# Hybrid decoder step on one core: output projection by contraction blocks over eight open tiles, w_ada piece 12 ahead of w_in, caches behind it

## Chip, cores and metric

One NeuronCore of a Trainium2 chip. The metric is the device time of one launch in microseconds. The kernel was timed in three runs; beside them stands one profiled execution, from which all durations are read. In the text TensorE is PE, VectorE DVE, ScalarE ACT, GpSimd POOL and SyncE SP, as in the rows.

## What is computed

One decoder layer in float32 for 256 prompt tokens and 8 decode tokens (264 columns), D = 1024:

```python
mod = silu(c) @ w_ada + b_ada                    # six vectors of 1024 for each condition row
h = rmsnorm(x, g_mix) * (1 + sc1) + sh1
q_a, k_a, v_a, q_h, f_h, i_h, g_h = split(h @ w_in)
o_a = rmsnorm(sink_attention(rotary(q_a), rotary(k_a), v_a))       # 8 heads, 2 KV heads, window 128
o_h = rmsnorm(hgrn(q_h, f_h, i_h)) * silu(g_h)                      # 4 heads, state 128 x 128
x = x + gt1 * (concat(o_a, o_h) @ w_out)
h = rmsnorm(x, g_ffn) * (1 + sc2) + sh2
x = x + gt2 * moe(h)                             # top 4 of 32 experts, clamped SwiGLU
y = rmsnorm(x, g_final)
```

Beside y the kernel returns the window caches and the states, which are updated (decode) or final (prompt).

## The kernel before

The program is written by hand for each engine, in the order in which the engine runs it, with semaphores between the engines. It has two parts.

**The front** (to about 260 us) does everything up to the router. Weights come through `ring`, eight places of 8 KB a partition; `PLACES` gives the place of each chunk and SP issues the loads in a fixed order. w_ada comes in 8 + 16 chunks (`w_ada_rows(i)`, 16 pieces of 1 MB), w_in in pieces of 1 and 2 MB (`w_in_columns`), w_out in four chunks WO0 to WO3: two hold the rows of the attention half (four DMAs each), two those of the hg half (one DMA each). A load waits until its place is free: `chunks_used` counts chunks of w_in and later ones, `ada_used` chunks of w_ada that PE has used. POOL issues the small and the strided loads: caches, sinks, router bias, states, and the copies of the caches to the outputs. PE does the input projection in turns with w_ada chunks (L961), the levels of the recurrence (L1197), rotations (L1204) and attention queries (L1213), then scores, values and the recurrence.

**The output projection** has `cat`, 8 contraction steps of 128 rows: steps 0 to 3 are attention heads, 4 to 7 hg heads. `project(d)` makes one of eight output tiles (128 columns of w_out) of 264 tokens in one PSUM bank, over all 8 steps (L1456); `x1_column(d)` on DVE (L2069 to L2075) adds it to the residual, ACT squares and scales it (L833, L834), and `token_sums(d)` (L1468, L1472) adds it to router logits and sums of squares. `outer` (L1440) makes the decode states' updates, `update_states` (L2059) adds them on DVE. `att_ready` and `hg_ready` tell that the two halves of `cat` are normalised (`norm_values`, `norm_heads`); on ACT their inverse roots are Ln and Exp for the prompt (L805, L808) and Sqrt for the decode rows (L801).

**The expert loop** runs 16 pairs of experts. A pair has 12 chunks of 2 MB; eight buffers hold them (`big(c)`): 0 to 3 are the ring's places two by two, 4 and 5 lie in the arena, 6 over the decode states, 7 over the residual. The first eight are issued one by one as their memory comes free at the front's end; from chunk 8 on each waits until PE has used the chunk eight before (`load_later`):

```python
sp.wait_ge(chunks_used, turn2 * (2 * PER) + (PRE + n - BIGS + 1))
expert_chunk(n, (turn2 * 2 + n // PER) % PAIRS)
```

PE's first matmul on a chunk is the first of L1656.

Of the kernel before, what the change touches and what calls it, by code (L numbers as in the profile page):

```python
# [24 lines left out]
KT = D // P  # L25
S = 256
NB = 8
# [51 lines left out]
    6, 7, 0, 6, 7, 0, 6, 7, 0, 1, 6, 7, 0, 1, 6, 7) + (6, 7, 4, 5)  # L79
# [65 lines left out]
def hybrid_layer(nc, A, O):  # L145
    with ExitStack() as ctx:
# [236 lines left out]
        for name, b in (  # L383
# [37 lines left out]
        def _(sp):  # L421
# [50 lines left out]
            for i in range(6, 12):  # L472
                w_ada_rows(i)
            w_in_columns(Z0 + 7, 12)
            for i in range(12, 2 * N_ADA):
                w_ada_rows(i)
            w_in_columns(Z0 + 9, 15)
            for c in range(4):
                n = WO0 + c
                if c < 2:  # L480
                    sp.wait_ge(ada_used, 15 + c)
                    for i in range(2):
                        for g in range(KV):
                            sp.dma_start(two(chunk(n))[64 * g:64 * g + 64, i, :], w_out_a[2 * c + i, g]).then_inc(full[place(n)], 16)
                else:
                    sp.wait_ge(chunks_used, Z0 + 9)
                    sp.dma_start(two(chunk(n)), w_out_h[c - 2]).then_inc(full[place(n)], 16)
# [58 lines left out]
        def _(pool):  # L546
# [15 lines left out]
            pool.wait_ge(chunks_used, Z0 + 5)  # L562
# [78 lines left out]
        def _(act):  # L641
# [185 lines left out]
            root(r_att[:, S:NTOK], "asd", bank("asd")[:, 0:NB], AW)  # L827

# [103 lines left out]
        def _(pe):  # L932
# [37 lines left out]
            give(mm, "cT")  # L970
            def turn_x(k):
# [457 lines left out]
            give(turn(out[:, 0:64], pvr[0:64, :], 64), "dT")  # L1429
            pe.wait_ge(sem("hg_squares"), 3)  # L1430
# [16 lines left out]
            def project(d):  # L1447
                out = take(f"wo{d}")
                for k in range(KT):
                    if d == 0:  # L1450
                        landed(WO0 + k // 2)
                        if k == 0:
                            pe.wait_ge(sem("att_ready"), 1)
                        if k == 4:
                            pe.wait_ge(sem("hg_ready"), 3)
                    mm = pe.matmul(out[:, 0:NTOK], lhsT=two(chunk(WO0 + k // 2))[:, k % 2, P * d:P * (d + 1)], rhs=cat[:, k, :],  # L1456
                                   start=(k == 0), stop=(k == KT - 1))
                give(mm, f"wo{d}")

            def token_sums(d):  # L1460
# [9 lines left out]
                if d == 6:  # L1470
                    mm.then_inc(chunks_used, 4)
# [18 lines left out]
            project(0)  # L1490
            project(1)
            outer(1, ("ow0", "ow1", "ow2", "ow3"))
            pe.wait_ge(sem("router_row"), 2)
            out = take("cwr")
            pe.matmul(out[:, 0:E], lhsT=ones[0:E, :], rhs=bdiag[0:E, :], start=True, stop=True)
            give(pe.matmul(out[0:NB, E:2 * E], lhsT=cw[0:E, 1:1 + NB], rhs=ident[0:E, 0:E], start=True, stop=True), "cwr")
# [209 lines left out]
        def _(dve):  # L1706
# [323 lines left out]
            dve.tensor_scalar(bdiag[0:E, :], ident[0:E, 0:E], cw[0:E, 0:1], None, ALU.mult).then_inc(sem("router_row"), 1)  # L2030
            wait_emptied(dve, "qkb")
# [13 lines left out]
            norm_heads(0)  # L2045
            norm_values(0, S)
            norm_heads(1)
            wait_emptied(dve, "asd")
            link(dve.reciprocal(r_att[:, S:NTOK], r_att[:, S:NTOK]))
            norm_values(S, NB).then_inc(sem("att_ready"), 1)  # L2050
            wait_emptied(dve, "hsd")
            link(dve.reciprocal(r_hgd, r_hgd))
            dve.tensor_tensor(cat[:, 4:8, S:NTOK], cat[:, 4:8, S:NTOK], r_hgd, ALU.mult).then_inc(sem("hg_ready"), 1)

# [7 lines left out]

            dve.wait_ge(sem("states_full"), 16 * NB)
            update_states(0, ("ou0", "ou1", "ou2", "ou3"))

# [11 lines left out]
            x1_column(0)  # L2077
            x1_column(1)
            update_states(1, ("ow0", "ow1", "ow2", "ow3"))
            wait_filled(dve, "cwr")  # L2080
            dve.tensor_copy(brow, bank("cwr")[:, 0:E])
            dve.tensor_copy(brow_s[0:NB, :], bank("cwr")[0:NB, E:2 * E]).then_inc(emptied("cwr"), 1)
            for d in range(2, KT):
                x1_column(d)
# [248 lines left out]
```

## Time and profile before

| | us |
|---|---|
| median of 3 runs | 1194.55 (1194.54 to 1194.88) |
| profiled execution, time | 1195.86 |
| its span, first to last instruction | 1194.1 |
| PE busy in the span | 1109.4 (93%) |
| DVE / ACT / POOL busy | 335.9 / 165.7 / 55.6 |
| DMA | 461.65 MB, mean 387 GB/s |
| mean granted clock of PE | 0.985 of 2.4 GHz |

The profile's page cuts the span into 40 slices of 30 us. The DMA moved 167 to 350 GB/s in slices 2 to 8 and about 430 from slice 11 to the last but one. Busy time is the time with an instruction running, whether or not it waits for a pipeline; what an engine waited for stands in the rows behind a bracket, as idle time and what ended it. A float32 matmul that is no transpose counts twice in the trace (16 projection matmuls are x32).

### The profile page before, as it was taken

What the parts mean: (1) busy time and instruction counts of PE and PEld (TensorE: products, weight loads), DVE (VectorE), ACT (ScalarE), POOL (GpSimd) and SP (SyncE); (2) the same over time, 40 slices, a digit from 0 to 9 for tenths busy, and PEclk for the clock granted to TensorE, in tenths of its full rate; (3) what the DMA queues carried; (4) which work ended last, traced back from release to release, by engine and by line L of the source; (5) the groups of instructions that cost most, each with busy time, mean ns of one, the idle gap of its engine ahead of it and who ended that gap; (6) DMA issues with size and microseconds to landing.
All of it is one profiled execution on the core that took longest, in us unless ns stands there. A gap on an engine that the chain in (4) does not pass through costs nothing.

```text
span 1194.1 us, 14038 instructions
## 1 busy us (share of the span) xinstructions
PE 1109.4 (93%) x5465; PEld 439.8 (37%) x5465; DVE 335.9 (28%) x753; ACT 165.7 (14%) x317; POOL 55.6 (5%) x86
## 2 busy tenths in 40 slices
PE   7997999999999999989898989898989898989896
PEld 3554577753332333323232323232323232323222
DVE  4133545351322232222222221212121212121214
ACT  3230153230010101000100010001000100000003
POOL 1111201210000000000000000000000000000000
PEclk9997998999999999999999999999999999999999
DMA  9879554689999999999999999999999999999994
GB/s 364 296 306 350 167 194 175 232 313 397 430 428 430 431 430 430 430 430 430 431 431 431 428 431 430 430 432 431 429 431 430 430 431 431 429 430 429 431 430 194
DMA packets 49128, 461.65 MB, mean 387 GB/s; under 512 B 6657, under 2 KB 7873, under 8 KB 22202
## 3 DMA queue, kind: packets, MB, share of 16 engines
q1 hardware_dynamic: 42512, 445.17, 89.2%
q0 software_dynamic: 5600, 13.13, 3.2%
q10 hardware_dynamic: 986, 2.95, 0.7%
q8 instruction: 20, 0.33, 0.1%
q14 instruction: 10, 0.08, 0.0%
HBM read 460.30 MB, written 5.78 MB: 390 GB/s over the span
## 4 chain that ended last, share of the span: by engine, by line
PE 57%; DMA 40%; DVE 2%; issue 1%; POOL 0%; ACT 0%; SPq 0%; DVEq 0%
PE bank L1656 27%; DMA arena<-in_w_up 17%; DMA ring<-in_w_up 17%; PE bank L1536 6%; PE bank L1680 4%; DMA ring<-in_w_ada 3%; DMA arena<-in_w_down 3%; PE bank L1456 3%; PE bank L937 2%; PE bank L1649 2%; PE bank L1116 1%; PE bank L1248 1%; PE bank L1039 1%; PE bank L1056 1%; PE bank L1542 1%; PE bank L961 1%
## 5 line engine op out<-in xcount | busy, mean ns | idle before, releaser
L1656 PE MATMUL bank<-arena 128*64 128x512 f32 x1024 | 240.0, 600 | 11.4 <-DMA arena<-in_w_up 10.9
L1656 PE MATMUL bank<-ring,arena 128*64 128x512 f32 x1024 | 240.0, 601 | 9.9 <-DMA ring<-in_w_up 8.7
L1656 PEld LDWEIGHTS bank<-arena 128*64 128x64 f32 x1024 | 67.3, 136 | 164.4 <-issue 149.5
L1656 PEld LDWEIGHTS bank<-ring,arena 128*64 128x64 f32 x1024 | 66.0, 136 | 163.6 <-issue 137.5
L1680 PE MATMUL bank<-arena 128*64 128x512 f32 x512 | 114.6, 596 | 9.1 <-DMA arena<-in_w_down 9.1
L1680 PE MATMUL bank<-ring,arena 128*64 128x512 f32 x512 | 114.6, 596 | 9.1 <-DMA ring<-in_w_down 9.1
L2229 DVE TENSOR_SCALAR arena<-bank 128x256 f32<-128x256 f32 x64 | 24.2, 419 | 275.2 <-PE bank L1656 275.2
L1536 PE MATMUL bank<-arena,mods 128*128 128x512 f32 (+1 forms) x204 | 93.7, 630 | 0.9 <-DVE arena L2256 0.9
L891 ACT ACTIVATE arena<-arena 128x512 f32<-128x512 f32 x32 | 20.2, 630 | 493.6 <-DVE arena L2229 493.6
L2218 DVE TENSOR_TENSOR x<-x,bank 128x512 f32<-128x512 f32 x64 | 44.0, 687 | 144.5 <-PE bank L1536 144.5
L937 PE MATMUL bank<-const,arena 128*128 128x128 f32 (+3 forms) x348 | 51.0, 288 | 23.2 <-DMA ring<-in_w_down 7.6
L2248 DVE COPY arena<-bank 64x512 f32<-64x512 f32 x30 | 20.6, 688 | 164.2 <-PE bank L1680 164.2
L1680 PEld LDWEIGHTS bank<-arena 128*64 128x64 f32 x512 | 36.4, 137 | 80.9 <-issue 69.6
L1680 PEld LDWEIGHTS bank<-ring,arena 128*64 128x64 f32 x512 | 35.2, 137 | 82.2 <-issue 61.5
L937 PEld LDWEIGHTS bank<-const,arena 128*128 128x128 f32 (+3 forms) x348 | 40.8, 165 | 54.8 <-issue 44.9
L612 POOL DMA_INDIRECT arena<-h_rows,idx x15 | 15.0, 998 | 810.4 <-DVE idx L2163 751.9
L1536 PEld LDWEIGHTS bank<-arena,mods 128*128 128x128 f32 (+1 forms) x204 | 22.8, 161 | 69.2 <-issue 68.7
L902 ACT ACTIVATE arena<-bank 64x512 f32<-64x512 f32 x32 | 18.9, 591 | 162.7 <-PE bank L1680 162.7
L1649 PE MATMUL bank<-arena 32*64 32x512 f32 x256 | 34.8, 613 | 0.0
L1456 PE MATMUL bank<-arena,ring 128*128 128x264 f32 x128 | 33.0, 417 | 1.2 <-DVE arena L2014 1.2
L898 ACT ACTIVATE arena<-bank 128x512 f32<-128x512 f32 x32 | 19.0, 595 | 79.0 <-PE bank L937 79.0
L1456 PEld LDWEIGHTS bank<-arena,ring 128*128 128x128 f32 x128 | 25.7, 205 | 8.1 <-issue 3.6
(338 smaller groups left out, 799.3 us busy)
## 6 DMA issues: line engine op xcount, KB each, us to landing
ring<-in_w_up SPq DMA_DIRECT2D x64, 2048.0 KB, 34.1
arena<-in_w_up SPq DMA_DIRECT2D x64, 2048.0 KB, 34.2
ring<-in_w_down SPq DMA_DIRECT2D x32, 2048.0 KB, 33.6
arena<-in_w_down SPq DMA_DIRECT2D x31, 2048.0 KB, 33.4
ring<-in_w_ada SPq DMA_DIRECT2D x16, 1024.0 KB, 10.1
ring<-in_w_ada SPq DMA_DIRECT2D x16, 512.0 KB, 10.9
ring<-in_w_in SPq DMA_DIRECT2D x3, 2048.0 KB, 12.8
ring<-in_w_in SPq DMA_DIRECT2D x5, 1024.0 KB, 12.4
```

The lines of the kernel that those rows point to most:

```text
L891: act.activation(sg, glu, ACT.Sigmoid, scale=ALPHA).then_inc(sem("sig_ready"), 1)
L898: act.activation(gT[e], B[6 + e][:, :], ACT.Copy).then_inc(sem("gT_copied"), 1)
L902: act.activation(ysb[r, e, :], B[4 + e][r, :], ACT.Copy).then_inc(sem("y_kept" if last else "y_copied_a"), 1)
L937: return pe.transpose(out, in_, ident[0:rows, 0:rows])
L1456: mm = pe.matmul(out[:, 0:NTOK], lhsT=two(chunk(WO0 + k // 2))[:, k % 2, P * d:P * (d + 1)], rhs=cat[:, k, :], start=(k == 0), stop=(k == ...
L1536: return pe.matmul(out, lhsT=Wc[:, cols], rhs=rows, start=first, stop=True, skip_group_check=True)
L1649: pe.matmul(B[2 * e + c % 2][64 * a:64 * a + 64, :], lhsT=own_row[32 * c:32 * c + 32, e, :], rhs=bias[32 * c:32 * c + 32, :], start=False, ...
L1656: mm = pe.matmul(B[2 * e + c % 2][64 * a:64 * a + 64, :], lhsT=xTe[:, k, 64 * e:64 * e + 64], rhs=big(PER * s + n)[:, r, 512 * c:512 * (c ...
L1680: mm = pe.matmul(B[4 + e][64 * a:64 * a + 64, :], lhsT=gT[e].rearrange("p (j a t) -> p j a t", j=4, a=2)[:, k % 4, k // 4, :], rhs=big(PER ...
L2218: dve.tensor_tensor(acc, acc, part, ALU.add).then_inc(sem("sum_added"), 1)
L2229: ins = dve.tensor_scalar(glu[:, 256 * b:256 * (b + 1)], u[:, :, 0], LIMIT, None, ALU.min)
L2248: dve.tensor_copy(ysb[dst, 1 - e, :], B[4 + e][src, :]).then_inc(sem("y_copied_d"), 1)
```

## The change

On SP, w_ada piece 12 is issued ahead of the w_in columns Z0+7 instead of behind them; w_out's hg half is issued ahead of its attention half, and the two halves trade places in the ring. Expert chunks 4 and 5 no longer wait for `hg_ready`; chunk 2 waits for 2 of the 4 counts that the projection gives, ahead of chunk 6. On POOL the caches and all behind them wait for the use of w_ada piece 12. On PE two 128x256 matmuls on constants are added at the front, the router-row matmuls ("cwr") move ahead of the decode norms, and the projection is done by contraction steps: 0 to 3 for tiles 0 to 3, outer products, 4 and 5 for tiles 0 to 3, 0 to 3 and then 4 and 5 for tiles 4 to 7, and 6 and 7 tile by tile with the token sums. The eight tiles have a bank each. On DVE and ACT the norms are put in another order.

```diff
-    6, 7, 0, 6, 7, 0, 6, 7, 0, 1, 6, 7, 0, 1, 6, 7) + (6, 7, 4, 5)
+    6, 7, 0, 6, 7, 0, 6, 7, 0, 1, 6, 7, 0, 1, 6, 7) + (4, 5, 6, 7)
...
-                ("wo0", 2), ("wo1", 3), ("ow0", 4), ("ow1", 5), ("ow2", 6), ("ow3", 7), ("cwr", 1), ("wo2", 2), ("rt", 0),
-                ("wo3", 3), ("wo4", 2), ("wo5", 3), ("h00", 4), ("h10", 5), ("wo6", 2), ("wo7", 3), ("h01", 4), ("h11", 5),
+                ("wo0", 0), ("wo1", 1), ("wo2", 2), ("wo3", 3), ("ow0", 4), ("ow1", 5), ("ow2", 6), ("ow3", 7), ("wo4", 4), ("wo5", 5),
+                ("wo6", 6), ("wo7", 7), ("rt", 0), ("h00", 4), ("h10", 5), ("h01", 4), ("h11", 5),
...
-            for i in range(6, 12):
+            for i in range(6, 13):
                 w_ada_rows(i)
             w_in_columns(Z0 + 7, 12)
-            for i in range(12, 2 * N_ADA):
+            for i in range(13, 2 * N_ADA):
                 w_ada_rows(i)
             w_in_columns(Z0 + 9, 15)
-            for c in range(4):
+            for c in (2, 3, 0, 1):
                 n = WO0 + c
                 if c < 2:
-                    sp.wait_ge(ada_used, 15 + c)
+                    sp.wait_ge(chunks_used, Z0 + 9)
...
                 else:
-                    sp.wait_ge(chunks_used, Z0 + 9)
+                    sp.wait_ge(ada_used, 13 + c)
...
             sp.wait_ge(sem("att_ready"), 1)
-            sp.wait_ge(sem("hg_ready"), 1)
             sp.wait_ge(sem("st_stored"), 16)
             for c in (4, 5):
                 expert_chunk(c, 0)
+            sp.wait_ge(chunks_used, PRE - 2)
+            expert_chunk(2, 0)
             sp.wait_ge(sem("states_stored"), 16 * NB)
             expert_chunk(6, 0)
             sp.wait_ge(chunks_used, PRE)
-            for c in (2, 3):
-                expert_chunk(c, 0)
+            expert_chunk(3, 0)
...
-            pool.wait_ge(chunks_used, Z0 + 5)
+            pool.wait_ge(ada_used, 13)
             pool.dma_start(vc, A["cache_v_win"][0].rearrange("b s g d -> s b (g d)")).then_inc(sem("cache_full"), 16)
...
-            inverse_root(r_hg[0])
             inverse_root(r_att[:, 0:S])
-            inverse_root(r_hg[1])
...
             root(r_att[:, S:NTOK], "asd", bank("asd")[:, 0:NB], AW)
+            inverse_root(r_hg[0])
+            inverse_root(r_hg[1])
...
+            for _ in range(2):
+                pe.matmul(B[1][:, 0:NEARLY], lhsT=ident, rhs=const[:, 0:NEARLY], start=True, stop=True)
...
-            project(0)
-            project(1)
+            for d in range(4):
+                project(d, 0, 4)
             outer(1, ("ow0", "ow1", "ow2", "ow3"))
...
+            for d in range(4):
+                project(d, 4, 6)
+            for d in range(4, KT):
+                mm = project(d, 0, 4)
+            release(mm, 2)
+            for d in range(4, KT):
+                project(d, 4, 6)
+            project(0, 6, KT)
+            project(1, 6, KT)
             token_sums(0)
-            for d in range(2, 6):
-                project(d)
+            for d in range(2, 7):
+                project(d, 6, KT)
                 token_sums(d - 1)
             for t in range(2):
                 turn_columns(f"h{t}0", x1s, t, 0, paired=True)
-            for d in range(6, KT):
-                project(d)
-                token_sums(d - 1)
+            project(7, 6, KT)
+            token_sums(6)
...
+            dve.wait_ge(sem("powers"), 1)
+            norm_values(0, S)
...
-            norm_heads(0)
-            norm_values(0, S)
-            norm_heads(1)
...
+            wait_filled(dve, "cwr")
+            dve.tensor_copy(brow, bank("cwr")[:, 0:E])
...
             dve.wait_ge(sem("states_full"), 16 * NB)
             update_states(0, ("ou0", "ou1", "ou2", "ou3"))
+            norm_heads(0)
+            norm_heads(1)
+            wait_emptied(dve, "hsd")
...
+            update_states(1, ("ow0", "ow1", "ow2", "ow3"))
```

SP's loads from w_ada piece 6 to expert chunk 7 (L464 are pieces of w_ada, L453 columns of w_in, L484 and L487 the two halves of w_out, L493 expert chunks), before:

```order
L464 DMA ring<-in_w_ada 128x2048 x6
L453 DMA ring<-in_w_in 128x8x512
L464 DMA ring<-in_w_ada 128x2048 x4
L453 DMA ring<-in_w_in 128x8x512
L484 DMA ring<-in_w_out 64x1024 x8
L487 DMA ring<-in_w_out 128x2x1024 x2
L493 DMA ring<-in_w_up 128x4096 x2
L493 DMA arena<-in_w_up 128x4096 x3
L493 DMA ring<-in_w_up 128x4096 x2
L493 DMA arena<-in_w_up 128x4096
```

and in the change:

```order
L464 DMA ring<-in_w_ada 128x2048 x7
L453 DMA ring<-in_w_in 128x8x512
L464 DMA ring<-in_w_ada 128x2048 x3
L453 DMA ring<-in_w_in 128x8x512
L487 DMA ring<-in_w_out 128x2x1024 x2
L484 DMA ring<-in_w_out 64x1024 x8
L493 DMA ring<-in_w_up 128x4096 x2
L493 DMA arena<-in_w_up 128x4096 x2
L493 DMA ring<-in_w_up 128x4096
L493 DMA arena<-in_w_up 128x4096
L493 DMA ring<-in_w_up 128x4096
L493 DMA arena<-in_w_up 128x4096
```

One w_ada piece went ahead of the w_in columns, the halves of w_out changed places, and an expert chunk in the ring went ahead of the one over the states.

PE from the decode norms (L1432, L1318) to the second token sums, before; L1440 are outer products, L1495 and L1496 the router row, L1456 projection matmuls:

```order
L1432 MATMUL bank<-arena,const 128x32
L1318 MATMUL bank<-arena,const 128x8 x4
L1440 MATMUL bank<-mods,arena 128x128 x16
L1456 MATMUL bank<-arena,ring 128x264 x16
L1440 MATMUL bank<-mods,arena 128x128 x16
L1495 MATMUL bank<-arena,const 128x32
L1496 MATMUL bank<-const,small 8x32
L1468 MATMUL bank<-arena,x 32x264
L1472 MATMUL bank<-arena,const 32x264
L1456 MATMUL bank<-arena,ring 128x264 x8
L1468 MATMUL bank<-arena,x 32x264
L1472 MATMUL bank<-arena,const 32x264
```

and in the change, where the router row is L1435 and L1436, the norms L1439 and L1321, outer products L1447, the projection L1464 and token sums L1478 and L1482:

```order
L1435 MATMUL bank<-arena,const 128x32
L1436 MATMUL bank<-const,small 8x32
L1439 MATMUL bank<-arena,const 128x32
L1321 MATMUL bank<-arena,const 128x8 x4
L1447 MATMUL bank<-mods,arena 128x128 x16
L1464 MATMUL bank<-arena,ring 128x264 x16
L1447 MATMUL bank<-mods,arena 128x128 x16
L1464 MATMUL bank<-arena,ring 128x264 x36
L1478 MATMUL bank<-arena,x 32x264
L1482 MATMUL bank<-arena,const 32x264
L1464 MATMUL bank<-arena,ring 128x264 x2
L1478 MATMUL bank<-arena,x 32x264
```

Between two token sums stand 2 projection matmuls now, 8 before.

ACT's inverse roots (L808), decode squares (L823, L825) and decode roots (L801) up to the first tile's squares (L833), before:

```order
L808 ACT_TABLE_LOAD
L808 ACTIVATE x<-x 128x512
L808 ACTIVATE x<-x 128x256
L808 ACTIVATE x<-x 128x512
L823 ACTIVATE arena<-arena 128x4x8
L825 ACTIVATE arena<-arena 128x4x8
L801 ACT_TABLE_LOAD
L801 ACTIVATE x<-bank,small 128x32
L801 ACTIVATE x<-bank,small 128x8
L833 ACTIVATE arena<-arena 128x264
```

and in the change, where the squares are L821 and L823:

```order
L808 ACT_TABLE_LOAD
L808 ACTIVATE x<-x 128x256
L821 ACTIVATE arena<-arena 128x4x8
L823 ACTIVATE arena<-arena 128x4x8
L801 ACT_TABLE_LOAD
L801 ACTIVATE x<-bank,small 128x32
L801 ACTIVATE x<-bank,small 128x8
L808 ACT_TABLE_LOAD
L808 ACTIVATE x<-x 128x512 x2
L833 ACTIVATE arena<-arena 128x264
```

The two hg roots stand behind the decode roots with a table load of their own; a further load stands ahead of the router's square roots (L856), where there was none.

## Rows read from the trace of the kernel before

**Rows 1.** Busy time by stretch: PE, PEld, DVE, ACT, POOL; PEclk, DMA share, GB/s.

```profile
264.00:285.00 21.00, 21.00 (x87) 5.59 (x85) 6.22 (x11) 0.63 (x1) 1.04 (x2) 1.00 0.98 370
450.00:1170.00 720.00, 666.58 (x3004) 214.99 (x3004) 167.49 (x327) 62.20 (x104) 10.89 (x11) 1.00 1.01 430
```

**Rows 2.** DMA issues at 183 us and at 264 us, to landing.

```profile
ring<-in_w_up SPq DMA_DIRECT2D x1, 2048.0 KB, 7.8
...
ring<-in_w_down SPq DMA_DIRECT2D x1, 2048.0 KB, 8.9
```

**Rows 3.** Timeline of PE, 93 to 132 us: start, us, line, tiles, [idle before].

```profile
95.35 1.92 PE L961 MATMUL bank<-ring,arena 128*32 128x512 f32 x16
...
103.34 1.06 PE L961 MATMUL bank<-ring,arena 128*32 128x512 f32 x8
113.24 1.93 PE L961 MATMUL bank<-ring,arena 128*32 128x512 f32 x8 [8.83 <-DMA ring<-in_w_ada]
...
125.42 1.93 PE L961 MATMUL bank<-ring,arena 128*32 128x512 f32 x16
```

**Rows 4.** Busy time by stretch, columns as in rows 1.

```profile
113.00:124.00 11.00, 10.76 (x48) 6.51 (x50) 4.21 (x8) 1.06 (x1) 0.00 (x0) 0.51 0.31 130
199.00:209.00 10.00, 8.81 (x52) 7.29 (x52) 9.03 (x30) 1.46 (x3) 0.57 (x1) 0.50 0.56 206
210.00:247.00 37.00, 36.84 (x222) 27.00 (x221) 13.38 (x63) 9.17 (x23) 6.36 (x9) 1.00 0.59 206
```

**Rows 5.** Timeline of SP's DMA issues, 80 to 90 us.

```profile
85.19 1.28 SPq L464 DMA_DIRECT2D ring<-in_w_ada  x3
86.51 1.10 SPq L453 DMA_DIRECT2D ring<-in_w_in  x1
89.34 3.26 SPq L464 DMA_DIRECT2D ring<-in_w_ada  x1
```

**Rows 6.** Timeline of POOL, 84 to 110 us, and DMA issues to landing.

```profile
85.46 0.95 POOL L563 DMA_DIRECT2D arena<-in_cache_v_win  x1 [25.97 <-PE bank L1213]
...
small<-in_attn_sinks POOLq DMA_DIRECT2D x8, 0.0 KB, 10.8
```

**Rows 7.** Timeline of DVE, 110 to 160 us.

```profile
118.88 0.70 DVE L1852 COPY_PREDICATED arena<-const,bank 128x512 f32<-128x512 uint32 x1 [14.81 <-PE bank L1197]
...
147.31 0.17 DVE L1905 TENSOR_TENSOR small<-small 128x8 f32<-128x8 f32 x1
```

**Rows 8.** Timeline of PE, 183 to 264 us.

```profile
203.54 10.13 PE L1456 MATMUL bank<-arena,ring 128*128 128x264 f32 x32 [1.19 <-DVE arena L2014]
...
219.87 3.83 PE L1456 MATMUL bank<-arena,ring 128*128 128x264 f32 x16
...
243.59 0.41 PE L1472 MATMUL bank<-arena,const 128*32 128x264 f32 x1
...
260.11 3.65 PE L1656 MATMUL bank<-ring,arena 128*64 128x512 f32 x16 [0.44 <-ACT arena L880]
```

**Rows 9.** Timeline of PE, 0 to 24 us.

```profile
10.54 0.47 PE L937 MATMUL bank<-const,arena 128*128 128x128 f32 x1 [0.49 <-DMA arena<-in_hg_lb_logits]
```

**Rows 10.** Timeline of DVE, 183 to 215 us.

```profile
200.34 1.67 DVE L2014 SCALAR_TENSOR_TENSOR arena<-arena,small,x 128x256 f32<-128x256 f32 x4
...
202.75 0.64 DVE L2014 SCALAR_TENSOR_TENSOR arena<-arena,small,x 128x8 f32<-128x8 f32 x4
...
203.91 4.22 DVE L2059 SCALAR_TENSOR_TENSOR arena<-arena,bank 128x128 f32<-128x128 f32 x16
```

**Rows 11.** Timelines of DVE and ACT, 215 to 240 us: tile 2.

```profile
219.41 0.48 DVE L2069 SCALAR_TENSOR_TENSOR arena<-bank,arena 128x256 f32<-128x256 f32 x1 [0.21 <-PE bank L1456]
...
220.53 0.49 ACT L834 ACTIVATE arena<-arena 128x256 f32<-128x256 f32 x1
```

**Rows 12.** Timeline of ACT, 183 to 264 us.

```profile
198.62 1.28 ACT L801 ACT_TABLE_LOAD   x1
...
245.19 0.26 ACT L856 ACTIVATE small<-bank,small 128x2 f32<-128x2 f32 x1 [0.55 <-PE bank L937]
```

More of the change, by code:

```diff
@@ L1429, in _ @@
             give(turn(out[:, 0:64], pvr[0:64, :], 64), "dT")
+            pe.wait_ge(sem("router_row"), 2)
+            out = take("cwr")
+            pe.matmul(out[:, 0:E], lhsT=ones[0:E, :], rhs=bdiag[0:E, :], start=True, stop=True)
+            give(pe.matmul(out[0:NB, E:2 * E], lhsT=cw[0:E, 1:1 + NB], rhs=ident[0:E, 0:E], start=True, stop=True), "cwr")
             pe.wait_ge(sem("hg_squares"), 3)
@@ L1445, in _, with project @@
             outer(0, ("ou0", "ou1", "ou2", "ou3"))
[L1447 to L1450, printed above, removed]
+            def project(d, first, last):
+                out = take(f"wo{d}") if first == 0 else bank(f"wo{d}")
+                for k in range(first, last):
+                    if d == 0 and k % 2 == 0:
                         landed(WO0 + k // 2)
[L1452 to L1455, printed above, removed]
+                    if d == 0 and k == 0:
+                        pe.wait_ge(sem("att_ready"), 1)
+                    if d == 0 and k == 4:
+                        pe.wait_ge(sem("hg_ready"), 3)
                     mm = pe.matmul(out[:, 0:NTOK], lhsT=two(chunk(WO0 + k // 2))[:, k % 2, P * d:P * (d + 1)], rhs=cat[:, k, :],
-                                   start=(k == 0), stop=(k == KT - 1))
-                give(mm, f"wo{d}")
+                                   start=(k == 0), stop=(k == KT - 1), skip_group_check=True)
+                if last == KT:
+                    give(mm, f"wo{d}")
+                return mm
             def token_sums(d):
@@ L1470, in token_sums @@
                 if d == 6:
-                    mm.then_inc(chunks_used, 4)
+                    mm.then_inc(chunks_used, 2)
                 mm = pe.matmul(out[E:2 * E, 0:NTOK], lhsT=ones[:, 0:E], rhs=squares_1[:, d % 4, :], start=(d == 0), stop=(d == KT - 1),
@@ L1488, in turn_columns @@
                     give(mm, name)
-            project(0)
-            project(1)
+            for d in range(4):
+                project(d, 0, 4)
             outer(1, ("ow0", "ow1", "ow2", "ow3"))
[L1493 to L1496, printed above, removed]
+            for d in range(4):
[7 more added lines that the diff above has]
+            project(1, 6, KT)
             token_sums(0)
-            for d in range(2, 6):
-                project(d)
+            for d in range(2, 7):
+                project(d, 6, KT)
                 token_sums(d - 1)
@@ L2044, in _ @@
             dve.tensor_tensor(km, wide(krows.unsqueeze(1), 1, NB), wide(C("same").unsqueeze(2), 2, P), ALU.mult).then_inc(sem("km_ready"), 1)
-            norm_heads(0)
-            norm_values(0, S)
-            norm_heads(1)
[L2048 to L2053, printed above, removed]
             def update_states(i, names):
@@ L2061, in update_states @@
                     ins.then_inc(emptied(names[hd]), 1)
+            wait_filled(dve, "cwr")
+            dve.tensor_copy(brow, bank("cwr")[:, 0:E])
+            dve.tensor_copy(brow_s[0:NB, :], bank("cwr")[0:NB, E:2 * E]).then_inc(emptied("cwr"), 1)
+            wait_emptied(dve, "asd")
+            link(dve.reciprocal(r_att[:, S:NTOK], r_att[:, S:NTOK]))
+            norm_values(S, NB).then_inc(sem("att_ready"), 1)
             dve.wait_ge(sem("states_full"), 16 * NB)
             update_states(0, ("ou0", "ou1", "ou2", "ou3"))
+            norm_heads(0)
+            norm_heads(1)
+            wait_emptied(dve, "hsd")
+            link(dve.reciprocal(r_hgd, r_hgd))
+            dve.tensor_tensor(cat[:, 4:8, S:NTOK], cat[:, 4:8, S:NTOK], r_hgd, ALU.mult).then_inc(sem("hg_ready"), 1)
+            update_states(1, ("ow0", "ow1", "ow2", "ow3"))
             def x1_column(d):
@@ L2075, in x1_column @@
                 dve.tensor_tensor(x1s[:, d, S:NTOK], xT[:, d, S:NTOK], s2T[:, d, 1:9], ALU.mult).then_inc(sem("x1s_ready_s"), 1)
[L2077 to L2083, printed above, removed]
+            for d in range(KT):
                 x1_column(d)
```

2 rows, old and new, of the table bank_of are left out of this document.

## The prediction

> **What bounds the kernel now.** I read the busy table of two stretches first. From 450 us to nearly the end the DMA engines are full (share 1.01, 430 GB/s) and TensorE is busy only 666.58 of 720 us: it waits for experts' weights. Between 264 and 285 us, just behind the start of the expert loop, it is the other way round: TensorE is busy all the time and the DMA moves 370 GB/s [rows 1]. The DMA list says why. Eight buffers of 2 MB hold experts' weights, and chunk 8 can be asked for only when TensorE has used chunk 0. The one asked for behind 263 us lands 8.9 us later; one that had the DMA nearly to itself, at 183, took 7.8 us [rows 2]. So almost nothing is queued when the loop starts, and from there 184 chunks come one behind the other: the end is the loop's start plus a constant. **What moves the loop's first matmul (260.11 us [rows 8]) moves the end by as much; what only lets weights land earlier ahead of it moves nothing.**
>
> So I read TensorE's list ahead of 260 us for time that is not work. The largest piece is a wait of 8.83 us, up to 113.24, for a piece of w_ada [rows 3]. Behind it the granted clock is at its lower level, 1.2 GHz: 0.51 from 113 to 124 us. A second low stretch, 0.50 from 199 to 209 us, lies around the start of the output projection [rows 4], which TensorE starts 1.19 us late, waiting for VectorE [rows 8].
>
> **The missed piece.** SyncE issues three pieces of w_ada at 85.19, 2 MB of w_in at 86.51 and the missed piece, w_ada 12, behind it at 89.34 [rows 5]. POOL starts 1 MB of caches at 85.46 [rows 6], and behind them sinks and 1 MB of copies in DRAM. In the change the piece goes ahead of w_in, and the caches wait until TensorE has used it. Four pieces of 1.05 MB from 85.2 us, at 400 GB/s (between the two rates of [rows 1]), take 10.5 us; with some 3 us of latency (7.8 less 4.9 for 2 MB [rows 2]) the piece lands by 99. TensorE wants it at 104.4 (103.34 and 1.06 [rows 3]). The pieces behind it are asked for when chunks 9, 10 and 11 are used, as before.
> The gain is the wait, 8.83 us, and the slow clock behind it. From 95.35 to 103.34 TensorE did two pieces, a level, a rotation and queries in 7.99 us at full clock; one piece less (0.93) is 7.06. From 113.24 to 125.42 it took 12.18 for that [rows 3], 5.12 more. Together **-13.95 us**. VectorE doesn't take the stall over: it waited 14.81 us for TensorE's next level meanwhile [rows 7].
>
> **What is moved down.** POOL's queue is released at about 105.3 instead of 85.46. Two caches and ten small issues at 0.95 us at most, and 10.8 us to landing [rows 6], put the sinks at 128. VectorE wants them at 147.31 [rows 7], in the change 13.95 earlier, at 133.4: 5 us to spare. The states behind them on POOL wait for an inner product of TensorE that moves by 13.95 too. On SyncE the hg half of w_out now comes first, and the attention half, 8 DMAs, waits for the first state product; behind it stand expert chunks 0 and 1, wanted only in the loop. No term.
>
> **The two matmuls at the front.** They have 256 columns each; by the projection's (8 of 264 columns in 3.83 us [rows 8]) that is 0.95 us together. TensorE waited 0.49 us for a load just behind [rows 9], which hides half. Bounds 0 and 0.95; I take **+0.4**.
>
> **The projection.** VectorE does the prompt's attention values (1.67 us) ahead of the decode rows' steps, and the two hg scalings (0.7 each, as between the two rows of values) behind the first state update. The decode values' end, att_ready, was 203.39 [rows 10]; without two scalings ahead it is 202.0. TensorE's outer products ended at 202.35 (203.54 less 1.19 [rows 8]) and come 0.4 later, for the values ahead of them. So the projection starts at about 202.8, **0.7 earlier**. The first state update (4.22 us [rows 10]) and the scalings end by 208.5 and are wanted behind 16 matmuls, at 213; the second update, behind the second outer products, ends by 218.3, and the first tile of the second four, at 217.9, needs only its first quarter.
> The 64 matmuls are the same. But before, a whole tile (3.83 us) lay between a tile's end and its sums; now 2 matmuls do, 0.95 us. From a tile's end (VectorE starts 0.1 behind it, at 219.41) to ScalarE's scaled column (221.02) are 1.7 us [rows 11]. Step by step, with 0.6 for a pair of sums: the first pair waits 0.8, tiles 2 and 4 0.25 each, and tile 6 0.55, because ScalarE copies two banks (0.5 each, as its column [rows 11]) ahead of its column: **+1.85**. The two router-row matmuls move into a gap, **-0.5** (at most 0.95 by the projection's). At the last sums (243.59 before [rows 8]) this comes to **+0.65**; bounds -1.2 with no waits, and +1.9 with neither the start nor the gap.
>
> **The tables of ScalarE.** Its two hg roots (Exp) now come behind the Sqrt of the decode rows, which adds two table loads of 1.28 us [rows 12]. The first ends before 203.4, covered by the 4.22 us of state update; without that cover its 1.28 would show in the second block. The second stands ahead of the router's square roots at 245.19, which had waited 0.55 us for TensorE [rows 12]. It hides this much and adds **+0.7** to the way to the loop; bounds 0 and 1.28.
> The Trainium skill (ScalarE: Activation LUTs, What ACT_TABLE_LOAD costs) speaks against such an order: it wants calls grouped by table and gives some 2.66 us for a switch, a drain included. By that the sum would be 1.38 higher. The rows show a load of 1.28 us alone, and they decide.
>
> **DMA behind the block order.** Chunk 2 can be issued when eight tiles have used the attention half, chunks 4 and 5 1.4 us earlier, chunk 6 in order behind chunk 2, chunk 3 where it was. All lie ahead of the first release at 264, where nobody waits for them: 0. Chunk 7 stays tied to the last transposes.
>
> **Sum.** -13.95 + 0.4 + 0.65 + 0.7 = -12.2. The profiled execution took 1195.86 us, 1.31 above the median of the runs, 1194.55: it would take 1183.7, and on the runs' scale **1182.4 us**.
>
> **Rivals.**
> *The second slow stretch shrinks.* Without the 1.19 us ahead of the projection the clock may stay up or come back sooner. Between 203.54 and 209 some 5.4 us ran at half: -2.7, 1179.7. Against: the waits ahead of 199 stay. 0.13.
> *It gets longer, or part of the stall stays* (the low clock through the rest of the first 16 matmuls, 4.6 us to 213.67 [rows 8]; or another piece late). About 1187. For: the low stretch behind 113 lasted over 10 us [rows 4]. 0.13.
> *The DMA is the bound already,* and the change does not bring what it moves: an earlier loop only waits for chunks. 1194.5. Against: 370 GB/s and 8.9 us behind the start [rows 1, 2]. 0.03.
> *Slower: the clock falls in the last block.* TensorE pauses there between tiles and goes through eight open banks. Its work is eight tiles of 0.95 and 0.6 us, 12.4; at the lower level 12.4 more, less the 1.85 of waits that it swallows, +10.5: 1192.9. If it lasts through the 16.5 us from the last sums to the loop [rows 8], of which I take a third as TensorE's own, +5.5: 1198. It ends on the slow side from 12.2 us of TensorE work at the lower clock. Against: from 210 to 247 us, with the same matmuls, the clock was 1.00 [rows 4], and the four pauses are under 1 us each. 0.06.
> The Trainium skill (TensorE: Matmul & The Clock Gate, A second HAM failure mode) tells of kernels whose groups cycle through PSUM banks with short pauses, and whose clock then swings; by that rule it would be this rival. The trace of before, which pauses less there, does not show it.
>
> **Numbers.** The forecast has 0.63; 0.02 is left for what I don't see. The range goes from the first rival less its small terms' bounds, 1178.6, to the second with the table's bound, 1188.0; it leaves out the other two. About 0.2%, 2.4 us, is what a measurement of this kernel can tell from no change. Faster 0.93, same 0.03, slower 0.04.
>
> **What would show it.** No wait for w_ada over 1 us on TensorE and a granted clock of 1.00 from 104 to 124 us; the loop's first matmul some 12 us before 260.11; short waits of the sums for ScalarE at the projection's end; a table load ahead of the router's roots; landing times near 8 us at the loop's start. I am wrong if the first matmul moves by 12 us and the end by much less (a queue at the DMA after all), if VectorE's maxima wait for the sinks, or if the clock is at 0.5 anywhere from the second block to the loop.

## The result and the profile after

The changed kernel took 1181.41 us (median of four runs, 1178.35 to 1182.54) beside 1194.55 of the kernel before, a ratio of 0.9887 with a 95% interval of 0.9867 to 0.9908. Six later runs gave 1182.34 and 0.9899 (0.9881 to 0.9916). The forecast was 1182.4. The profiled execution took 1182.54 us, its span 1180.7.

TensorE's timeline from 94 us on, of the changed kernel, answers to [rows 3] and [rows 8] (start, us, line, tiles, [idle before]):

```profile
94.81 1.92 PE L961 MATMUL bank<-ring,arena 128*32 128x512 f32 x16
102.80 1.92 PE L961 MATMUL bank<-ring,arena 128*32 128x512 f32 x16
104.65 2.00 PE L1200 MATMUL bank<-arena 128*128 128x64 f32 x16
...
187.81 9.12 PE L1464 MATMUL bank<-arena,ring 128*128 128x264 f32 x32
...
215.27 0.38 PE L1478 MATMUL bank<-arena,x 128*32 128x264 f32 x1 [1.02 <-DVE arena L2093]
227.20 0.38 PE L1478 MATMUL bank<-arena,x 128*32 128x264 f32 x1 [0.75 <-ACT arena L834]
229.05 0.39 PE L1482 MATMUL bank<-arena,const 128*32 128x264 f32 x1
235.26 1.60 PE L1539 MATMUL bank<-arena,const 128*128 128x32 f32 x12 [2.50 <-DVE arena L2124]
239.04 7.77 PE L1569 MATMUL bank<-mods,arena 128*128 128x128 f32 x48
247.68 3.65 PE L1670 MATMUL bank<-ring,arena 128*64 128x512 f32 x16 [0.44 <-ACT arena L880]
```

The missed piece is one of the 16 records at 102.80, and no wait is left there. The loop starts at 247.68 instead of 260.11, 12.43 earlier (forecast 12.2). The stretches, with the columns of [rows 1] and [rows 4]:

```profile
104.00:124.00 20.00, 20.00 (x137) 12.00 (x130) 11.82 (x23) 3.79 (x6) 13.97 (x22) 1.00 0.82 297
184.70:191.30 6.60, 6.60 (x46) 5.63 (x46) 5.14 (x21) 3.76 (x6) 0.00 (x0) 0.50 0.63 207
192.00:236.00 44.00, 39.55 (x232) 28.75 (x230) 17.89 (x77) 13.54 (x30) 7.94 (x11) 1.00 0.70 259
236.00:243.00 7.00, 7.00 (x41) 5.43 (x41) 6.15 (x24) 1.17 (x2) 2.22 (x5) 0.53 0.41 122
450.00:1150.00 700.00, 648.29 (x2918) 208.90 (x2917) 161.75 (x314) 59.97 (x100) 10.88 (x11) 1.00 1.01 430
```

The clock is up from 104 to 124, where it was 0.51 for 11 us. It is at the lower level for 6.6 us around the projection's start (10 before, [rows 4]), and for most of 236 to 243, in the router's work behind the projection. There the kernel before had 3.4 us of it, behind a wait of 1.79:

```profile
249.26 1.34 PE L1525 MATMUL bank<-arena,const 128*128 128x32 f32 x12 [1.79 <-DVE arena L2112]
```

```profile
250.50:253.50 3.00, 3.00 (x20) 1.90 (x19) 2.86 (x8) 1.07 (x2) 0.00 (x0) 0.50 1.02 437
```

The steady stretch has the same 430 GB/s.

ScalarE's timeline behind the projection answers to [rows 12], POOL's and SP's at the missed piece to [rows 6] and [rows 5]:

```profile
229.88 1.28 ACT L856 ACT_TABLE_LOAD   x1
231.18 0.26 ACT L856 ACTIVATE small<-bank,small 128x2 f32<-128x2 f32 x1
```

```profile
105.05 0.95 POOL L563 DMA_DIRECT2D arena<-in_cache_v_win  x1 [45.58 <-PE bank L961]
```

```profile
84.65 4.48 SPq L464 DMA_DIRECT2D ring<-in_w_ada  x4
89.17 0.43 SPq L453 DMA_DIRECT2D ring<-in_w_in  x1
```

The table load stands ahead of the roots, the caches start 20 us later, and the four pieces go ahead of w_in.

To compare kernels, TensorE's way to the loop is cut at three rows. A is the start of the last pair of w_ada pieces ahead of the missed one's (95.35 in [rows 3], 94.81 above), B the time from there to the projection, C from there to the last sums (the last of their rows: 243.84 before, 0.25 behind the one in [rows 8]; 229.05 above), D from there to the loop's first matmul, E the rest of the span. Each line is one profiled execution; the median is that of the kernel's runs, and the ratio is to runs of the kernel before beside them.

| kernel | A | B | C | D | E | median us | ratio, interval |
|---|---|---|---|---|---|---|---|
| before | 95.35 | 108.19 | 40.30 | 16.27 | 933.99 | 1194.55 | 1 |
| changed | 94.81 | 93.00 | 41.24 | 18.63 | 933.02 | 1181.41 | 0.9887 (0.9867 to 0.9908) |
| changed again | 95.10 | 93.40 | 41.70 | 17.10 | 933.40 | 1182.34 | 0.9899 (0.9881 to 0.9916) |
| piece and caches alone | 92.28 | 94.19 | 39.41 | 14.87 | 936.35 | 1178.88 | 0.9872 (0.9854 to 0.9890) |
| piece alone | 94.36 | 104.10 | 40.53 | 16.33 | 933.38 | 1188.86 | 0.9952 (0.9933 to 0.9971) |
| caches alone | 91.81 | 94.20 | 39.39 | 14.87 | 933.73 | 1176.26 | 0.9863 (0.9837 to 0.9888) |
| the rest alone | 91.90 | 105.95 | 40.35 | 18.42 | 933.18 | 1196.11 | 1.0010 (0.9993 to 1.0028) |
| hg roots together | 92.44 | 92.66 | 40.19 | 17.87 | 933.54 | 1176.07 | 0.9844 (0.9815 to 0.9872) |
| busy wait | 94.50 | 93.17 | 41.06 | 15.66 | 933.41 | 1181.31 | 0.9895 (0.9878 to 0.9913) |
| half blocks | 90.73 | 93.25 | 37.59 | 17.28 | 933.55 | 1178.56 | 0.9874 (0.9856 to 0.9892) |
| half blocks, roots | 94.58 | 92.95 | 38.62 | 17.85 | 933.30 | 1174.99 | 0.9835 (0.9788 to 0.9881) |
| half blocks, roots, busy | 93.57 | 93.25 | 38.28 | 15.18 | 934.92 | 1174.91 | 0.9831 (0.9813 to 0.9849) |
| changed, warm front | 90.31 | 93.25 | 40.31 | 18.41 | 933.22 | 1177.24 | 0.9881 (0.9858 to 0.9904) |
| all together | 90.19 | 92.66 | 37.43 | 15.04 | 933.58 | 1172.05 | 0.9834 (0.9802 to 0.9866) |

C and D hold two things: the work, and how long the clock was low in it. TensorE is busy for nearly all of C (40.14 of 40.30 us before, 39.29 of 41.24 in the changed kernel), so the time at the lower level (0.50) may be counted half. That time is 5.6 us of C before, 3.6 in the changed kernel and 1.6 in "half blocks". Counted half, it leaves C at full clock: 37.5 us in all four profiles without blocks, 39.5 in all six with eight open tiles, 36.8 in all four with half blocks, each within 0.05. What C differs by otherwise is the clock.

### The profile page after: what moved, and what is told of

Same layout as the page of the kernel before. It is cut to its first block, busy times and chain, and to the rows that moved or that the text cites. A ratio compares the mean times of both kernels' runs of the same rounds, so it can differ in the third digit from the quotient of the medians.

```text
span 1180.7 us, 14048 instructions
## 1 busy us (share of the span) xinstructions
PE 1105.9 (94%) x5469; PEld 439.2 (37%) x5469; DVE 335.9 (28%) x753; ACT 168.3 (14%) x319; POOL 55.6 (5%) x86
## 4 chain that ended last, share of the span: by engine, by line
PE 62%; DMA 35%; DVE 2%; issue 1%; ACT 0%; SPq 0%; ACTq 0%; DVEq 0%
PE bank L1670 28%; DMA arena<-in_w_up 17%; DMA ring<-in_w_up 14%; PE bank L1550 6%; PE bank L1694 5%; PE bank L937 3%; DMA arena<-in_w_down 3%; PE bank L1464 3%; PE bank L1663 2%; PE bank L1119 2%; PE bank L961 1%; PE bank L1059 1%; PE bank L1216 1%; PE bank L1251 1%; PE bank L1042 1%; PE bank L1200 1%
## 5 line engine op out<-in xcount | busy, mean ns | idle before, releaser
L1464 PE MATMUL bank<-arena,ring 128*128 128x264 f32 x128 | 32.3, 408 | 0.0
L1464 PEld LDWEIGHTS bank<-arena,ring 128*128 128x128 f32 x128 | 24.9, 200 | 6.6 <-issue 2.4
```

## The experiments

**Piece and caches, each alone and both.** The kernel before, with one edit of the change or two:

```diff
-            for i in range(6, 12):
+            for i in range(6, 13):
...
-            pool.wait_ge(chunks_used, Z0 + 5)
+            pool.wait_ge(ada_used, 13)
```

> The kernel before with the missed piece ahead of w_in and the caches behind it, and nothing else of the change. Theory (the stall and its slow clock are the whole gain, the projection's part costs a little): the loop's first matmul comes 14 to 14.6 us before 260.11, at about 245.5 to 246, and the time is 1180 to 1181 us, as fast as the whole change or up to 2 us faster. Rival (the contraction in blocks brings a share of the gain): over 1184 us, and a loop start behind 249.

Both together take B from 108.19 to 94.19, 14.00 less (the terms of the stall and its slow clock said 13.95). C and D fall too, by 0.89 and 1.40. The low clock around the projection's start lasts as long as before, 10.2 us, but begins 6.4 us ahead of the projection instead of 4.6, so that less of it lies in C; in D the clock stays at 1.00. At 1178.88 this is no slower than the whole change. Its loop started at 240.75, earlier than expected, partly because A was 3.07 shorter; its E is 1.4 to 3.3 longer than all the others, which stays unexplained.

> The kernel before with the piece ahead of w_in alone; the caches stay where they were. Theory (the sum on record: four pieces of 1.05 MB, here with 1 MB of caches and 1 MB of copies beside them, 6.2 MB at 400 GB/s from 85.2 us and 3 us of latency, so landed by 98 to 104 us; TensorE wants the piece at about 104): the wait for w_ada is under 1 us, the clock stays up, and the time is within 1 us of the kernel with both moves, about 1180.5. Rival (the caches are what delays the piece): a wait of 2 us or more with the clock at its lower level behind it, 1184 to 1192 us.

This expectation missed: 1188.86, the rival's range. TensorE's timeline with the piece alone:

```profile
102.35 1.92 PE L961 MATMUL bank<-ring,arena 128*32 128x512 f32 x16
...
114.49 1.06 PE L961 MATMUL bank<-ring,arena 128*32 128x512 f32 x8 [4.08 <-DMA ring<-in_w_ada]
116.94 1.94 PE L961 MATMUL bank<-ring,arena 128*32 128x512 f32 x8 [1.38 <-DMA ring<-in_w_ada]
118.80 3.68 PE L1197 MATMUL bank<-arena 128*128 128x64 f32 x16
```

The piece itself is in time, at 102.35. The next two, which SP issues at 95.48, are late by 5.46 us together: the stall has moved on to them, and the clock has fallen behind it (3.68 us for the level's 16 matmuls, 2.00 at full clock).

> The kernel before with the caches behind the missed piece alone; the piece stays behind w_in. Theory (what lies ahead of the piece decides, 3 pieces, 2 MB of w_in and the piece are 6.3 MB, 15.7 us at 400 GB/s and 3 us of latency from 85.2: landed at about 104): a wait of 0 to 2 us is left in place of 8.83, and the time is 1180 to 1186 us, by whether the clock falls. Rival (w_in ahead of the piece is the whole delay): a wait of 5 us or more and 1188 to 1194 us.

This one missed too, on the good side: 1176.26 in place of 1180 to 1186. The caches alone do it, with no wait, and B, C and D as with both. So it is the caches and copies in the middle of the stream of pieces that made one late, and the piece's place ahead of w_in adds nothing to the time once they are gone. Which of the queue's transfers does it was not tried: all of them moved together. The margin is thin. The piece is issued at 85.80, as before behind w_in, and lands 14.6 us later (23.9 before), at 100.4; TensorE wants it 0.3 us later, in the middle of the row at 99.80. In the changed kernel it lands at 97.0 and is wanted at 103.7. TensorE's timeline with the caches alone:

```profile
99.80 1.92 PE L961 MATMUL bank<-ring,arena 128*32 128x512 f32 x16
101.66 2.00 PE L1197 MATMUL bank<-arena 128*128 128x64 f32 x16
...
186.01 9.22 PE L1456 MATMUL bank<-arena,ring 128*128 128x264 f32 x32 [0.99 <-DVE arena L2014]
...
230.83 1.22 PE L1525 MATMUL bank<-arena,const 128*128 128x32 f32 x12 [1.80 <-DVE arena L2112]
...
233.29 6.10 PE L1555 MATMUL bank<-mods,arena 128*128 128x128 f32 x48
```

The 48 matmuls of the router's stretch take 6.10 us here, 7.77 in the changed kernel.

**The rest alone.** The changed kernel with those two hunks undone, the signs turned.

> The changed kernel with the piece and the caches back in their old places: the contraction in blocks, the order of w_out, the tables and the front matmuls alone. Theory (they cost a little): the wait of about 8.8 us for w_ada and the slow clock behind it are back, the last sums come within 0.7 us of 243.59, the loop starts at 260 to 262.5, and the time is 1194.5 to 1197 us, by the terms on record 1196.3. Rival (the blocks bring a gain of their own): under 1193 us.

As expected by the time, 1196.11, no gain: the stall is back (8.70), D is 18.42. The loop's start, 256.62, is earlier than expected, because A is 3.45 and B 2.24 less than before. The rows behind the stall show most of B's part:

```profile
109.66 1.94 PE L961 MATMUL bank<-ring,arena 128*32 128x512 f32 x8 [8.70 <-DMA ring<-in_w_ada]
...
120.58 1.92 PE L961 MATMUL bank<-ring,arena 128*32 128x512 f32 x16
```

From the missed piece to the next pair it is 10.92 us, 12.18 before: the clock came back sooner, 1.26. With 0.13 from the wait, 0.85 is left for the projection's earlier start (forecast 0.7). So without the stall's cure the blocks are worth nothing; beside it they cost, by the rows of "changed" and "piece and caches alone", -1.19 in B, +1.83 in C and +3.76 in D, 4.40 together, and by those of "changed again" 3.73. Of D's 3.76, 3.4 is the clock, low there for 6.8 us in the one profile and not at all in the other. The intervals of the ratios overlap, so the runs alone do not show this cost.

**What D is made of.** First the order of ScalarE's roots put back:

```diff
+            inverse_root(r_hg[0])
+            inverse_root(r_hg[1])
             act.wait_ge(sem("o_ready"), 1)
...
-            inverse_root(r_hg[0])
-            inverse_root(r_hg[1])
```

> The changed kernel with ScalarE's two hg roots back ahead of the decode rows' roots, so without the two added table loads. The stretch from the last sums to the loop's first matmul took 18.63 us in the changed kernel, 16.27 before and 14.87 in the two runs without the stall and without the blocks. Theory (the loads cost what was measured, 0.5, and no more): 17.9 to 18.2 us, the wait ahead of the ranks' matmuls near 1.8 in place of 2.50, the clock low all the same behind it, and a time 0.5 to 0.7 us below the changed kernel's. Rival (the longer wait is what lets the clock fall): near 15 us, the clock at 1.00 through the stretch, 3 to 4 us faster. Second rival (the hg roots wait on the path at the projection's start): the projection starts later by up to 1 us and takes the gain back.

D lost 0.76 and the wait is 1.80 again, but the clock fell behind it all the same: the 12 matmuls take 1.87 us, 1.22 with the caches alone.

```profile
230.73 1.87 PE L1539 MATMUL bank<-arena,const 128*128 128x32 f32 x12 [1.80 <-DVE arena L2124]
```

So the length of this one wait does not decide. The runs gained more (1176.07) than these rows explain.

Then dummy matmuls in that wait:

```diff
-            pe.wait_ge(sem("chosen_ready"), 1)
             out = take("rank")
+            for _ in range(5):
+                pe.matmul(out[:, 256:512], lhsT=ident, rhs=const[:, 0:NEARLY], start=True, stop=True)
+            pe.wait_ge(sem("chosen_ready"), 1)
```

> The changed kernel with five dummy matmuls of 256 columns (some 2.3 us at the higher clock) in the wait of 2.50 us ahead of the ranks' matmuls; nothing is left out. Theory (TensorE's idle time there is what lets the clock fall): the granted clock stays at 1.00 behind it, the 48 matmuls take 6.1 us instead of 7.77, and the stretch from the last sums to the loop 15.5 to 16 us instead of 18.63: about 3 us faster than the changed kernel. Rival (the pauses of the last tiles, ahead of it, have decided already): the clock falls all the same, the dummies take up to 4.6 us and the stretch 18.6 to 21.

TensorE's timeline with them:

```profile
232.28 2.35 PE L1537 MATMUL bank<-const 128*128 128x256 f32 x10
234.95 1.22 PE L1541 MATMUL bank<-arena,const 128*128 128x32 f32 x12 [0.32 <-DVE arena L2126]
...
237.42 6.10 PE L1571 MATMUL bank<-mods,arena 128*128 128x128 f32 x48
```

The clock stays up, the 48 matmuls take 6.10 and D is 2.97 less, as the theory said. The median of the four runs is 1181.31 nevertheless, not below the changed kernel's. The profiled execution bears the theory out; a gain in the time is not shown.

**The thin last block.** Blocks for the first four tiles only, with SyncE's chunk 6 ahead of chunk 2:

```diff
             for d in range(4):
-                project(d, 4, 6)
...
+                project(d, 4, KT)
             token_sums(0)
...
+            project(4, 0, KT)
+            token_sums(1)
...
+            release(project(7, 0, 4), 2)
+            project(7, 4, KT)
             token_sums(6)
```

> The changed kernel with blocks for the first four tiles alone: their attention halves, the second outer products, their other halves, and then tiles 4 to 7 whole, one behind the other, with the sums a tile behind as before. Projection start to last sums took 41.24 us in the changed kernel, 39.4 in the runs without blocks and stall. Theory (the thin last block costs its waits, and its pauses let the clock fall behind it): 39 to 39.6 us, no wait of the sums over 0.2 us, and from the last sums to the loop 15 to 17 us instead of 18.63; together 3.5 to 5.5 us faster than the changed kernel, about 1176 to 1178. Rival (the wait of 2.50 us alone lets the clock fall): the stretch behind the last sums stays at 18 to 18.7 and only 1.8 us are gained.

C is 37.59, lower than the theory's range and 3.65 less than with all eight open; no sum waits more than 0.16. At full clock it is 2.7 less than with eight open tiles and 0.7 less than without blocks; the rest is that the clock was low for 1.6 us of it, 3.6 in the changed kernel. D stays above 17 and the clock falls in it, so the fall does not need the thin block. Next, this edit and that of the roots together:

> The same with the hg roots ahead of the decode rows' roots, so without the added table loads. Theory: another 0.5 to 0.7 us, the stretch from the last sums to the loop at 14.9 to 16.3 us, as without blocks, and the projection's start not later than in the changed kernel by more than 0.5: the fastest of the four, 1175 to 1177.5. Rival: the roots delay the decode rows' values and the projection starts up to 1 us later, so no gain against the run with loads.

The median, 1174.99, is in the theory's range, but the runs lie between 1170.87 and 1180.98. In the profile D is 17.85 with the clock at its lower level behind a wait of 1.80, the same wait behind which it stayed up in "caches alone".

And with dummies as above, `range(4)` in place of `range(5)`:

> Blocks for the first four tiles alone, the hg roots ahead of the decode rows' roots, and four dummy matmuls (1.9 us) in the wait ahead of the ranks' matmuls. Theory: from the pieces ahead of the missed one to the loop 93 us to the projection's start, 38 to 38.6 to the last sums and 14.9 to 15.2 to the loop: 146 to 147 us in place of 152.9, so some 6 us faster than the changed kernel on the same chip, about 1173 to 1176. Rival (the clock falls elsewhere in their place): over 149 us.

B, C and D add up to 146.71, as expected, and D is 15.18 with the clock up. But at the loop's start the first 16 matmuls take 5.35 us instead of 3.65, and E is 1.5 longer: the clock fell there instead. The median, 1174.91, does not differ from the kernel's without dummies.

**The front.** The changed kernel again, as it is, and with work for TensorE ahead of its first load (`zeros_made` is counted up by the clearing of `rest`):

```diff
+            pe.wait_ge(sem("zeros_made"), 1)
+            for _ in range(5):
+                pe.matmul(B[1][:, 0:NEARLY], lhsT=rest[:, 0:P], rhs=rest[:, 0:NEARLY], start=True, stop=True)
             pe.wait_ge(sem("ident_full"), 16)
```

> The changed kernel once more, beside the next two on the same chip. It is there for the spread of its runs and for a second profile of it. Theory (its runs differ by when the clock rises at the front: the modulation's first transposes of TensorE come at 21.2 to 21.9 us or at 24.8 to 25.2 in the profiles so far, 3.5 us apart): runs in two groups some 3.5 us apart, 1178 and 1182, and in the profile 152.9 us within 1 from the pieces ahead of the missed one (94.81 in the first profile) to the loop's first matmul. Rival (the spread comes of the weights' stream): the stretch from the loop's first matmul to the end differs by 3 us from 933.0.

> The changed kernel with five matmuls of 256 columns on cleared data from about 1.6 us on, while TensorE waits for its first constants up to 6.6; nothing is left out. Theory (the clock at the front rises after TensorE has been at work for some time, so work ahead of the first load brings it forward): the modulation's first transposes at 18 to 21.5 us in place of 25.2 or 21.3, the runs within 2 us of each other, and the median 2 to 5 us below the changed kernel's. Rival (the front waits for its loads, the pieces of w_ada): the transposes stay at 21 or later and the median is within 1.5 us.

Of the changed kernel again, five of six runs lie between 1181.63 and 1183.25 and one at 1177.33; E is as before, so the weights' stream is not what differs between profiles. Behind the same wait of 2.50 us the clock is low for 3.4 us this time, 6.8 in the first profile, and the 48 matmuls of the router's stretch take

```profile
239.85 6.54 PE L1569 MATMUL bank<-mods,arena 128*128 128x128 f32 x48
```

where they had taken 7.77; D is 1.53 less. The front of the changed kernel, and that with the early work:

```profile
7.53 2.07 PE L972 MATMUL bank<-const 128*128 128x256 f32 x4
...
16.34 1.94 PE L988 MATMUL bank<-ring,arena 128*32 128x256 f32 x16
...
25.22 0.44 PE L937 MATMUL bank<-const,mods 128*128 128x128 f32 x2 [0.51 <-ACT mods L650]
```

```profile
1.58 4.63 PE L967 MATMUL bank<-arena 128*128 128x256 f32 x10 [1.58 <-DVE arena L1735]
...
14.30 1.07 PE L991 MATMUL bank<-ring,arena 128*32 128x256 f32 x16
...
19.74 0.44 PE L937 MATMUL bank<-const,mods 128*128 128x128 f32 x2 [0.50 <-ACT mods L650]
```

The same 16 matmuls take 1.94 in one and 1.07 in the other, as at the clock's two levels, and the modulation's transposes come 5.5 us earlier; A is 4.50 less. But "half blocks", which has no early work, has the fast rate as early:

```profile
19.83 0.44 PE L937 MATMUL bank<-const,mods 128*128 128x128 f32 x2 [0.50 <-ACT mods L650]
```

Over the twelve profiles without early work these transposes lie between 19.83 and 25.33 us. The two with it (19.74 here, 19.61 below) are the earliest of all, but do not show by themselves that the early work is the cause. Four of the six runs are at 1176.2 to 1177.3, but two are at 1183.2; the intervals of the two ratios overlap. An effect on the time is likely and not shown.

The last kernel has both, the half blocks with roots and dummies and this front:

> The last kernel with the five matmuls on cleared data ahead of the first load as well. Theory: the pieces ahead of the missed one at 90.3 us as with the warm front alone, 93.25 from there to the projection, 38.3 to the last sums, 14.9 to 15.2 to the loop, 933.0 to 933.6 behind it (1.5 more if the clock falls at the loop's start again): a span of 1169.9 to 1172, a time of 1171.7 to 1173.8 and a median below both the changed kernel's and the last kernel's. Rival (a low stretch that is taken away at one place comes back at another): a median of 1175 or more, with the clock at its lower level somewhere between 180 us and the loop's start for longer than the 6 us around the projection.

TensorE's timeline of the last kernel:

```profile
19.61 0.44 PE L937 MATMUL bank<-const,mods 128*128 128x128 f32 x2 [0.50 <-ACT mods L650]
...
182.85 7.98 PE L1467 MATMUL bank<-arena,ring 128*128 128x264 f32 x32
...
223.74 1.89 PE L1539 MATMUL bank<-const 128*128 128x256 f32 x8
...
228.19 6.10 PE L1573 MATMUL bank<-mods,arena 128*128 128x128 f32 x48
235.32 3.65 PE L1674 MATMUL bank<-ring,arena 128*64 128x512 f32 x16 [0.60 <-ACT arena L880]
```

Five runs from 1170.67 to 1174.11, median 1172.05: every one below every run of the changed kernel. By its median it is the fastest here, 9 to 10 us ahead of the changed kernel, by the ratios 6 to 8; by the ratio it does not differ from the two kernels with half blocks and roots. A, B, C and D are as forecast within 0.9.

## Why the prediction was right, and where not

The total was right, and it rested on what it named: the loop's start moves the end. Over loop starts from 235.32 to 260.11 us E is 933.0 to 934.9 in all profiles but one (936.35). The DMA was no bound ahead of it; the chunk asked for at 251.59 landed 9.2 us later, 8.9 before [rows 2].

By the cuts, forecast against changed less before, and the same from the second profile of the changed kernel:

| | forecast | changed | changed again |
|---|---|---|---|
| A | +0.4 | -0.54 | -0.25 |
| B | -14.65 | -15.19 | -14.79 |
| C | +1.35 | +0.94 | +1.40 |
| D | +0.7 | +2.36 | +0.83 |
| sum | -12.2 | -12.43 | -12.81 |

In the first profile the sum is nearer than its parts, which is luck. (The range's upper end comes to 1187.6 by the terms it names, not 1188.0.)

- **The missed piece, -13.95: right** in size (-14.00 with its two edits alone), and it landed at 97.0 (forecast: by 99). The prediction did not say which edit carries it; the expectations did, and were wrong. Without the caches' move the next two pieces are 5.46 us late, and with that move alone the piece need not go ahead. What the caches cost the pieces behind the missed one was in neither.
- **What is moved down, no term: right.** POOL was released at 105.05 (forecast 105.3), and no engine on the way waited for it.
- **The two front matmuls, +0.4: it did not last.** They took 1.86 us, at the slow rate, and put the first w_ada matmuls at 12.83 (12.40 before), but the modulation's transposes stand at 25.22 and 25.23. A's -0.54 arises behind: a wait of 0.43 us for a w_ada piece, at 76.71 before, is not there. Between profiles A differs by up to 5 us by when the slow rate at the front ends (19.6 to 25.3 us for the modulation's transposes).
- **The projection, +0.65: its parts were mis-sized.** The start came 0.8 to 1.2 earlier than with piece and caches alone, not 0.7. The waits of the sums were 1.95 us together (1.02, 0.09, 0.09 and 0.75 by TensorE's timeline), 1.85 forecast. But C at full clock grew by 2.0, not 1.35; where the other 0.6 lies was not traced. Against it stands less slow clock in C, 3.55 us in place of 5.61, which gives back 1.0: the first rival come true at about a third of its 2.7. That makes C's +0.94.
- **The tables, +0.7: right for the load; what failed is the stretch around it, taken as fixed.** The load stands at 229.88, and the wait behind it grew from 1.79 to 2.50, 0.71. The rows show the load at 1.28 and the root 0.02 behind its end. The Trainium skill's larger price (ScalarE: Activation LUTs, What ACT_TABLE_LOAD costs, 2.66 us by its figures) is not what they show. D grew by 2.36 in the first profile because the clock was low for 6.8 us in place of 3.4 in it, which costs 1.7, and by 0.83 in the second, where it was low for 3.4 as before. In these profiles D is 14.9 to 15.7 us with the clock up and 16.3 to 18.6 where it falls.
- **The sign of being wrong that came true:** the clock was at 0.5 between the second block and the loop, in both profiles. It had been so in the kernel before as well (0.50 from 250.5 to 253.5), which the prediction did not read.
- **The rival of a slow clock** was put into the last block, and there the clock held 1.00 through its pauses. The Trainium skill (TensorE: Matmul & The Clock Gate, A second HAM failure mode) tells of a kernel that cycles through PSUM banks and whose clock swings by the short pauses between its groups; this block is no such case. The clock fell 7 us later. Work in the pause kept it up through D in all three profiles that had it, though in one it then fell at the loop's start; without, it stayed up in two and fell in nine. Whether it falls behind a given pause is not settled: the same wait of 1.80 us is followed by either.

## What to carry to other kernels

Where a load on a strict schedule is missed, look first for bulk transfers that share the DMA in those microseconds and are wanted late: moving 2 MB of them away did all of it here, while moving up the missed load alone made the next two late. Split a stretch by rows that every version has before crediting parts of a change: here one edit alone gained at least as much as the whole change, and the rest gave back 3.7 to 4.4 us by the profiles. And count TensorE's work at the clock of its stretch: a stretch behind a pause is not a fixed term, and two profiles of the same kernel can differ in it by more than the term in question (D 18.63 and 17.10).

## What was not expected

TensorE runs at half speed at the front as well. For up to 17 us, busy nearly all the time, it takes 1.94 us for matmuls that take 1.07 later. The profile's clock column says 1.00 from 6 to 24 us, but the trace's first record of the clock lies at 24.1 us (at 11.2 in the run with early work), so that this rests on the durations alone. In the two profiles with 4.63 us of work on cleared data ahead of the first load the modulation comes earliest of all, at 19.6 and 19.7 us, though one profile without it has 19.8. Between executions of one kernel the time differs by up to 10 us where its steady stretch does not. The slow front is a part of it, how long the clock is low around the projection and behind it is another, and the rest was not found.
